# Small steps between the panels' products, taken two at a time at half as many places (two attentions and the gated delta layer)

## What is computed (the reference, cut to what matters)

```python
# neighbourhood attention: local scores with bias beside context scores, one softmax
p = softmax(concat([s_loc, s_ctx])); out = p_loc @ v_win + p_ctx @ v_ctx
# forgetting attention
s = (q @ k.T) * scale + c_i[:, None] - c[None, :]
o = softmax(where(mask, s, NEG)) @ v;  o = o * sigmoid(og);  return o @ w_out
# gated delta rule, chunk by chunk
A = where(strict, (k @ k.T) * dec * beta, 0);  W, U0 = solve(A + I, [k*beta*exp(g), v*beta])
U = U0 - W @ S;  O = q_dec @ S + qk @ U;  S = g_last * S + U.T @ k_dec
O = rmsnorm(O) * silu(og);  return O @ w_out
```

## Time and profile before

| what | value |
|---|---|
| median of 3 runs | 2881.06 us |
| the profiled execution | 2876.47 us |
| its span, first to last instruction | 2874.7 us |
| mean granted TensorE clock | 0.942 |
| TensorE matmuls busy | 2626.7 us (91%) |
| weight loads busy | 2351.2 us (82%) |
| DVE, ACT, POOL busy | 1380.0, 985.9, 991.6 us |

### The profile page before, as it was taken

The page is one execution under the profiler, slowest core; times in us unless marked ns, Lnnn a source line. Parts: engine busy times, 40 slices in busy tenths (PEclk is TensorE's granted clock), DMA queues, the critical chain, the costliest instruction groups (busy, mean ns, idle before and its releaser), DMA issues.

```text
span 2874.7 us, 45814 instructions
## 1 busy us (share of the span) xinstructions
PE 2626.7 (91%) x19804; PEld 2351.2 (82%) x19804; DVE 1380.0 (48%) x2139; ACT 985.9 (34%) x1530; POOL 991.6 (34%) x585
## 2 busy tenths in 40 slices
PE   6999967899999799999899999888999988999997
PEld 4777756678888677777889999888889877999997
DVE  3545547363634434444264455456563433635464
ACT  4234343232323434344443333444232213333232
POOL 0643334644444212212524444500011213344444
PEclk8999988899999899999999999999999987999998
DMA  7532210333333211111212333312111001233321
GB/s 192 143 101 70 62 55 1 103 88 95 90 94 90 57 38 44 40 38 43 76 58 82 92 86 92 89 45 64 34 38 31 23 20 56 59 89 89 88 85 63
DMA packets 379930, 201.36 MB, mean 70 GB/s; under 512 B 6465, under 2 KB 377153, under 8 KB 379729
## 3 DMA queue, kind: packets, MB, share of 16 engines
q1 hardware_dynamic: 379728, 198.42, 24.6%
HBM read 196.30 MB, written 2.10 MB: 69 GB/s over the span
## 4 chain that ended last, share of the span: by engine, by line
PE 58%; DVE 21%; ACT 12%; issue 5%; POOL 3%; DMA 1%; SPq 0%; POOLq 0%; ACTq 0%; DVEq 0%
PE ps L625 41%; DVE t_ffy L2699 7%; ACT t_wh L593 4%; DVE t_ffy L2702 2%; ACT t_ffy L2606 2%; DVE t_atq L2499 2%; POOL t_wl L603 1%; PE ps L2316 1%; PE ps L2915 1%; DVE t_ffy L2708 1%; PE ps L2255 1%; PE ps L2289 1%; PE ps L1023 1%; PE ps L2934 1%; PE ps L476 1%
## 5 line engine op out<-in xcount | busy, mean ns | idle before, releaser
L603 POOL TENSOR_TENSOR t_wl<-t_raw,t_wh 128x1024 fp32r<-128x1024 f32 (+2 forms) x268 | 610.8, 2280 | 1070.5 <-ACT t_wh L593 1070.5
L593 ACT ACTIVATE t_wh<-t_raw 128x1024 fp32r<-128x1024 f32 (+2 forms) x323 | 327.8, 1016 | 666.1 <-PE ps L625 639.1
L625 PE MATMUL ps<-t_hh,t_wh 128*128 128x264 f32 (+2 forms) x2048 | 490.0, 319 | 18.7 <-ACT t_hh L2592 9.8
L625 PE MATMUL ps<-t_hh,t_wl 128*128 128x264 f32 (+2 forms) x2048 | 456.7, 302 | 3.5 <-POOL t_wl L603 3.5
L625 PE MATMUL ps<-t_hl,t_wh 128*128 128x264 f32 (+2 forms) x2048 | 451.8, 302 | 0.0
L625 PEld LDWEIGHTS ps<-t_hh,t_wh 128*128 128x128 f32 x2048 | 328.2, 195 | 47.3 <-issue 27.3
L625 PEld LDWEIGHTS ps<-t_hh,t_wl 128*128 128x128 f32 x2048 | 331.0, 195 | 15.1 <-POOL t_wl L603 3.9
L625 PEld LDWEIGHTS ps<-t_hl,t_wh 128*128 128x128 f32 x2048 | 326.4, 193 | 12.3 <-issue 5.5
L625 PE MATMUL ps<-t_fhh,t_wh 128*128 128x264 f32 (+1 forms) x1040 | 282.8, 326 | 9.8 <-DVE t_fhl L1666 5.2
L625 PE MATMUL ps<-t_fhh,t_wl 128*128 128x264 f32 (+1 forms) x1040 | 283.8, 327 | 4.7 <-POOL t_wl L603 4.6
L625 PE MATMUL ps<-t_fhl,t_wh 128*128 128x264 f32 (+1 forms) x1040 | 280.0, 325 | 0.0
(11 more groups left out here) (552 smaller groups left out, 4461.5 us busy)
## 6 DMA issues: line engine op xcount, KB each, us to landing
t_raw<-in_up SPq DMA_DIRECT2D x44, 512.0 KB, 3.9
t_raw<-in_up2a SPq DMA_DIRECT2D x44, 512.0 KB, 3.9
t_raw<-in_up2b SPq DMA_DIRECT2D x44, 512.0 KB, 3.9
t_raw<-in_attn_in SPq DMA_DIRECT2D x33, 512.0 KB, 4.1
t_raw<-in_dn_in SPq DMA_DIRECT2D x33, 512.0 KB, 4.1
t_raw<-in_ada_w SPq DMA_DIRECT2D x32, 512.0 KB, 4.2
t_raw<-in_w_in SPq DMA_DIRECT2D x25, 512.0 KB, 4.6
t_raw<-in_down SPq DMA_DIRECT2D x16, 512.0 KB, 3.8
```

Of the source, the lines that this page charges most:

```text
L593: ac.activation(wh[slot_of[j]][:, 0:kc, :], raw[r % NRAW][:, 0:kc, :], ACT.Copy).then_inc(up("wh_cut", "cut", j), 1)
L603: eng.tensor_tensor(wl[slot_of[j]][:, 0:kc, :], raw[r % NRAW][:, 0:kc, :], wh[slot_of[j]][:, 0:kc, :].bitcast(F), SUB).then_inc(up(name, " ...
L625: ins = pe.matmul(ps[bank_of(j, i)][:, 0:tn], wt[slot][:, k, :], a[:, k, t0:t0 + tn], start=first, stop=last)
```

## The change

`every` is doubled in the two attentions and the gated layer, and at each place two steps are put in place of one. The first place stays after product 2 (`every=6`) or 1 (`every=4`), so there are 4 places of two steps in 24 products (`every=6`), 6 of two (`every=4`), and 3 of two in 12. `tick` now returns what the generator yielded; `turn_max` yields `ALONE`, and no second step follows it when it is the first at its place. `fmul` of either G now waits (in the plan) until all of `og` is planned.

```diff
+        ALONE = 2
 ...
                 if went:
-                    return
+                    return went
 ...
-                if every and i % every == every - 1 and not ends:
+                if every and i % every == every // 2 - 1 and tick() != ALONE:
                     tick()
 ...
-        gemm(("xbc",), then_first, every=2)
-        gemm(("z",), then_first, every=2)
+        gemm(("xbc",), then_first, every=4)
+        gemm(("z",), then_first, every=4)
 ...
                     put("turn_max", p, banks=2)
-                    yield 1
+                    yield ALONE
 ...
-            gemm(("pair",), then_pair, keep=0, every=3, group=p)
+            gemm(("pair",), then_pair, keep=0, every=6, group=p)
 ...
-                gemm(("sig",), then_sig, keep=0, every=3, group=p - 1)
+                gemm(("sig",), then_sig, keep=0, every=6, group=p - 1)
 ...
-            gemm(("sig",), then_sig, keep=0, every=3, group=p)
+            gemm(("sig",), then_sig, keep=0, every=6, group=p)
 ...
-        NORMED, nstate, pads_after = set(), [0, 0], []
+        NORMED, OGS, nstate, pads_after = set(), set(), [0, 0], []
 ...
             put("froot", G)
             yield 1
+            while G not in OGS:
+                yield 0
             for e in range(4):
                 put("fmul", G, e, banks=2)
 ...
-        gemm(("qkv",), then_qkv, keep=0, every=3, group=1)
+        gemm(("qkv",), then_qkv, keep=0, every=6, group=1)
 ...
                 put("dog", m // 4)
+            if m == KD - 1:
+                OGS.update((0, 1))
 
-        gemm(("og",), then_og, keep=0, every=3)
+        gemm(("og",), then_og, keep=0, every=6)
 ...
-        gemm(("do",), None, every=2, group=0)
+        gemm(("do",), None, every=4, group=0)
```

## The result

The median of six executions of the changed kernel is 2863.59 us (2854.35 to 2869.96), that of the kernel before, run beside it, 2883.88 us: ratio 0.9927, 95% interval 0.9904 to 0.995. Faster by 0.73%, half of the 1.42% that were forecast, and inside the range. The profiled execution took 2864.04 us, 12.4 less than the one before. The medians are 20.3 us apart; the profiled execution of before is one of its shorter ones, 7.4 us under that median. What follows accounts for the 12.4 us of the two traces.

What follows compares the result with a forecast made beforehand. No one engine bounds the whole; most of the span is TensorE work and stages follow one another. 7.8 + 10.1 + 11.7 + 23.2 - 8.4 - 3 = 41.4 us off 2876.5, so 2840 for the median; range 2820 to 2866.

Steps and rivals of the forecast that it cites:

- term 2: Forgetting attention: gain 10.1 us, 6.1 from shorter waits of `weights`, 2.4 and 1.6 from pairs (bounds 4 to 17).
- term 5: Gated layer: new waits lose 8.4 us at 12 places where both steps are one worker's, and 3 us in `qkv`.
- term 1: Neighbourhood attention: 12 steps a panel fit into `xbc`, so the 6.0 us wait goes; gain 7.8 us (bounds 4 to 10).
- Gated layer, pairs: Gated layer: 39 places with two 64 by 64 steps save 0.3 us each, 11.7 us (bounds 0 to 12.9).
- Uncovered steps: Gated layer: 28 more steps fit between products, fewer stand uncovered after `do`, more after `og`; gain 23.2 us.
- The tail: Gated layer's end, after `do`: 25 uncovered steps, an excess of 22.3 us, of which nothing of the workers is left.
- The middle: Gated layer between `og` and `do`: 14 uncovered steps in place of 5, 22 us, excess 7.3 after 8.2 before.
- its own refutation: Prediction wrong if TensorE's idle time in `qkv` and `og` grows over 20 us, or the clock there falls below 0.9.
- A (only the covered tail): Rival: standing together saves nothing on TensorE, terms of 11.7, 2.4 and 1.6 fall away; 2856 us, chance 0.18.
- B: Rival: gated layer's middle, in-pair waits and low clock take more, forgetting attention's pairs bring nothing; 2862 us, chance 0.12.
- C (slower): Rival, all pairs: DVE's handlers of a pair queue behind one another, 0.3 us at each of 193; 2898 us, chance 0.05.
- D: Rival: TensorE's time is conserved, waits saved in `drain` come back in `do`; same time, 2878 us, chance 0.05.

Runs made afterwards that it cites:

- Experiment 1: The changed kernel with the same steps and order, each step alone at one of twice as many places: 2881.92 us, ratio 1.0002.
- second trace of before: The kernel before the change, nothing altered, run and traced once more: 2873.47 us.
- experiment 3: The kernel before the change with the last two `weights` of each pair of heads at one place: 2865.72 us, ratio 0.9945.
- experiment 2: The changed kernel with `turn_max` ahead of the two `mixing`: 2832.53 us, ratio 0.9814; the same order in the kernel before: 2877.64 us, ratio 0.9994.

## Why the prediction was half right

Of the 26.3 us by which the three stages missed, 13.3 are the forgetting attention's, and the step that failed there is in term 2: "covered by the 12 products", and 0.8 us less for `weights` in each of groups 1 to 4. It was to win 6.1 us of waits for `turn_max`; they grew by 10.3. The second is term 5, the new waits of the gated layer, whose 11.4 us left out the half clock behind them. That the total still lies inside the stated range is in part luck: the pairs of B and the wait at `values` won some 12 us that the forecast did not have, against this loss.

**Neighbourhood attention (7.8, measured 4.9).** The 6.0 us wait and its half clock went as forecast: the clock column fell 3.2 us. The step that failed is that term 1 has nothing for new waits. "Pairs here mix the 64-row scores with full-array steps and save nothing" is true of the rest column, but the second step of a place now waits 0.6 to 0.8 us for ACT, nine times. Experiment 1 prices that at 6.7 us. Three of the nine are what term 5 looked for in the gated layer, a second step that needs the handler of the first; in the other six ACT's copy stands behind an exp that is late. Neither was looked for here.

**Forgetting attention (10.1, measured -3.2).** The pairs were under-priced: 4.0 forecast, 7.9 to 10.2 measured. I had read "two in a row change shape as often as before" from the shapes; from product to product two `row_max` together save about 0.2. The waits failed. "In groups 5 and 6 ... is covered by the 12 products": the twelve products were counted, the queues they pass weren't. `turn_max` was moved behind the panel's end, and so ACT's copies behind the square, DVE's evacuation and the reciprocal of `pair_norm`: 4.2 us where nothing was expected. In groups 1 to 4 `weights` wait 2.54 in place of the 1.2 forecast, and the multiply under POOL's cut is 1.5 of it; in group 7 they wait 2.54 where nothing was expected. Waits for `turn_max`: +10.3 us against -6.1 forecast, and 10.2 at half clock with them (17.1 against the second trace of before, so the loss in this stage is 3.2 or 8.2 us). On the other side 7.3 us at `values` came unforeseen, from an exp and its table loads (experiment 3). In the changed kernel a change of order alone takes both away (experiment 2); in the kernel before the same order wins nothing, as other waits take the place of these.

**Gated layer, pairs (11.7).** Right: 10.9 us of rest (experiment 1).

**Uncovered steps (23.2).** The tail came as forecast: the end took 20.4 us in place of 67.2, `do` 66.4 in place of 71.4 with more steps in it; the waits and the clock from `do` on fell by 8.8 and 13.7, 22.5 us for a forecast excess of 22.3. The middle was over-priced: 22 us forecast for the 14 steps, 16.2 measured, at full clock. With four `fmul` and both workers in turn, hardly a step waits (2.3 us in all). Before, 5.1 us of it were waits and clock: 2.8 won there, for 0.9 forecast.

**New waits (-8.4 and -3).** Under-priced: from `ua` to the last product of `og` the waits grew by 10.2 us and the clock's share by 10.3. The clock was the part left out. TensorE's idle time there is within the bound that the prediction gave as its own refutation (20), and the clock (0.92) too, so these rows alone would not have shown it wrong. How much of the clock's share is the plan's is less sure than the sum: in the second trace of before this stretch lost 6.8 us in place of 11.9, and `do` and what follows 32.9 in place of 29.7.

The sum for the gated layer, by columns: rest 8.5, middle 2.8, from `do` on 22.5, `qkv` and `og` -20.5, together 13.3 for the 13.4 measured. Against the forecast the new waits are 9.1 worse, the middle 1.9 better, and the rest 3.2 short of 11.7: 0.8 for the pairs, and 2.4 that the same steps cost more between products than in a row (369.3 with single steps spread out, 366.9 before), which were priced alike.

**The rivals.** A (only the covered tail) is refuted: the pairs count on TensorE, in C as forecast. B has the nearest time (2862), and its mechanism, waits and a low clock, is where the gated layer lost (in `qkv` and `og`, not in the middle); that the forgetting attention would lose by its order no rival had. C (slower) is refuted as one mechanism, since the 145 pairs of B and C bring 19.9 us of rest. D is what experiment 1 shows for single steps: more of them per panel win nothing.

## What to carry to other kernels

In the gated layer and the forgetting attention the same small steps cost 8 to 11 us less of TensorE's work in pairs than one by one, and in the gated layer less was lost at half clock. In the neighbourhood attention pairs saved 1.1 us and brought 6.7 of waits, so that the steps one by one were 5.9 us shorter. Decide it stage by stage. When a step moves past the end of a panel, write out for each engine what its handler stands behind; the products in between are no cover if the handler waits in another queue. And look at which function each ACT instruction needs: moving one exp out from between two square roots won three quarters of what this whole change did.

## What the runs showed that I had not expected

- Half clock that outlasts its wait: some 27 us in a row with single steps, in both traces, behind one wait of 1.61 us, and 8.5 to 27.4 us ahead of `do` for one and the same plan. Most of the spread between executions is this: 149 to 185 us in all for the kernel before, while the span times the clock stays between 2707 and 2720.
- Waits and clock often fall together: 14.5 us of waits less in experiment 2, 22.2 us of clock; 7.3 and 10.3 (or 3.4, by the second trace of before) in experiment 3. But with `turn_max` first in the kernel before, 3.6 us of waits went and the clock's 15.4 stayed.
- Two steps of 64 by 64 tiles can run into one another: `uy` with `uf` at one place takes 1.10 us, where each alone takes 0.80. In the timeline their matmuls alternate.

```profile
2298.62 0.27 PE L2920 MATMUL ps<-t_dT,t_dAT 64*64 64x64 f32 x2
2298.67 0.22 PE L2954 MATMUL ps<-t_dT,t_dAT 64*64 64x64 f32 x1
2298.68 0.22 PE L2920 MATMUL ps<-t_dT,t_dAT 64*64 64x64 f32 x1
2298.73 0.45 PE L2954 MATMUL ps<-t_dT,t_dAT 64*64 64x64 f32 x5
```
- A DVE multiply of 0.71 us takes 2.19 when it starts during POOL's cut.
